# Feed forward of a three-layer fp32 block kernel: gate and up products as seven quarter products and sums, with the weight sums on GpSimd and VectorE

## Chip, cores and metric

One Trainium2 chip, one of its NeuronCores. The metric is the device time of one execution in microseconds (us). Everything is float32. Engines are named as in the profile: PE is TensorE (its weight loads, PEld, are listed apart), DVE is VectorE, ACT is ScalarE, POOL is GpSimd, SP is SyncE, which here issues the weight transfers.

## What is computed

The whole program is two layers of attention, gating and a mixture of experts, then a second kind of block over 256 tokens of width 1024. The change touches the last part of that block alone, the feed forward:

```python
h = rmsnorm(x, pre_ffn_g[l])
gt = causal_dwconv(h @ w_ff_gate[l], ff_conv_w[l]) + ff_conv_b[l]
y = (jax.nn.gelu(gt, approximate=True) * (h @ w_ff_up[l])) @ w_ff_down[l]
x = x + rmsnorm(y, post_ffn_g[l])
```

`h` is 256 tokens by 1024, `w_ff_gate` and `w_ff_up` are 1024 by 2816, `w_ff_down` is 2816 by 1024. The convolution goes over the tokens, with three taps, each column by itself.

## The kernel before, in words

The gate and up weights come in 11 chunks (`UP_CHUNKS`) of 2 MB, each 256 columns of the gate matrix and the 256 columns of the up matrix that belong to them, for all eight 128-row pieces of the depth (`KD`). They go in turn into four ring slots. SP issues the load into a slot when the last product of the chunk that lay there is done (`last_read` in the sync block). The normed tokens lie transposed in `x2T` (128 partitions, 8 depth pieces, 256 tokens).

In `feed_forward` of the tensor block a chunk is four products into four banks of PSUM, `A[0]`, `V[0]`, `A[1]`, `V[1]` (gate and up, for each of two 128-column halves `f`), each of eight matmuls of 256 tokens. An fp32 matmul stands as two PE instructions in the trace, so a chunk is 64 of them. ScalarE copies each gate bank to `gate_in`, VectorE runs three convolution operations per half into `conved` (L3044 to L3046), ScalarE applies the GELU (L2084), and VectorE multiplies by the up bank into `hidden` (L3053). ScalarE loads a table whenever it goes from copying to GELU or back.

After the 11 chunks the down products (L1571) run over `hidden` in six chunks of up to four tiles, into the banks `S[0]`, `S[1]`, `V[2]`, `V[3]`. Ahead of the feed forward stands `mixed_norm`: VectorE norms the rows (L3027, behind a power that GpSimd computes, L3095), PE transposes them (`turn_mixed`, L1302), ScalarE and VectorE write `x2T`. GpSimd has nothing to do during the feed forward; its last two powers belong to the norm at the very end. Each engine runs its own instructions in the order in which they are written, and semaphores alone hold the engines together.

Of the kernel before, what the change touches and what calls it, by code (L numbers as in the profile page):

```python
# [21 lines left out]
P = 128  # L22
# [261 lines left out]
def emit(nc, ctx, t, out):  # L284
# [15 lines left out]
    def count(name):  # L300
        return Count(nc, ctx, name)
# [25 lines left out]
    def col(name, l=None):  # L327
        a, n = COLS_AT[name if l is None else f"{name}{l}"]
        return cols[:, a:a + n]
# [98 lines left out]
    mix_g, ffn_g = heads[:, 5632:6656], heads[:, 6656:7680]  # L428
    gate_in = work[:, 0:2 * (SEQ + 2)].rearrange("p (b n) -> p b n", b=2)
    conved = work[:, 1024:1536].rearrange("p (b n) -> p b n", b=2)  # L430
    wr_flat = wr[:, :, :, :].rearrange("p l k n -> p (l k n)")
    w_alow = wr_flat[:, 0:KD * GLA_RANK].rearrange("p (k n) -> p k n", k=KD)
    w_alpha = wr_flat[0:GLA_RANK, 128:384]
# [109 lines left out]
    o2sq_done = count("o2sq_done")  # L543
    y_gla_done = count("y_gla_done")
    conv_done, gelu_done = count("conv_done"), count("gelu_done")
    x_done = count("x_done")
    dve_step = count("dve_step")
    out_stored = sem("out_stored")
# [3 lines left out]
    names = ("list", "weights", "rows", "pe", "act", "dve", "index", "gate", "sent", "passed")  # L552
    xb = [{n: sem(f"further_{n}{l}") for n in names} for l in range(DEPTH)]
    mark = {}

    def h_done_mix(l):
        return sum(2 * tiles(k) for k in range(l + 1))
# [5 lines left out]
    def at_bank(b):  # L563
        return (b.full, b.fills)

    def let_go(b):
        return (b.free, b.fills)
# [27 lines left out]
    def _(pe):  # L595
        def slot_of(c):
            s, n = AT[c]
            pe.wait_ge(ring_loaded[s], 16 * (n + 1))
            return ring[s]
# [4 lines left out]
        def emptied(*banks):  # L604
            for b in banks:
                pe.wait_ge(b.free, b.fills)
# [688 lines left out]
        def turn_mixed(tile):  # L1295

            for q, b in enumerate((S[tile], V[tile])):
                pe.wait_ge(*((xhat_done.sem, NT * DEPTH + 2 + tile + 1) if q else (xhat_half.sem, 2 + tile + 1)))
                pe.wait_ge(b.free, b.fills)
                for j in range(4):  # L1300
                    f = 4 * q + j
                    mm = pe.transpose(b.t[:, j * P:(j + 1) * P], x2hat[:, tile, f * P:(f + 1) * P], ident)  # L1302
                mm.then_inc(b.full, b.fill())
                mark["mixed_T", tile, q] = at_bank(b)

        def columns2(name, banks, between=None):
            w = slot_of(("in2", 2, name))
# [230 lines left out]
            mark["attended", 2] = at_bank(S[0])  # L1538

        def feed_forward():  # L1540
            mark["up"] = [b.fills for b in A + V]

            def chunk(q, loaded):
                s = AT["up", 2, q][0]
                pe.wait_ge(ring_loaded[s], loaded)
                for f in range(2):
                    for part_, b in ((0, A[f]), (1, V[f])):
                        pe.wait_ge(b.free, b.fills)
                        for k in range(KD):
                            c0 = k * COLS + part_ * 256 + f * P  # L1550
                            mm = pe.matmul(b.t[:, 0:SEQ], ring[s][:, c0:c0 + P], x2T[:, k, :], start=(k == 0), stop=(k == KD - 1))  # L1551
                        mm.then_inc(b.full, b.fill())

            n_turn = UP_CHUNKS // NSLOT
            turns = Turns(*[(b, "fills", NSLOT) for b in (A[0], A[1], V[0], V[1])])
            with pe.Fori(0, n_turn) as i:
                turns.turn(i)
                for q in range(NSLOT):
                    chunk(q, 16 * (AT["up", 2, q][1] + 1) + 16 * i)
            turns.done(n_turn)  # L1560
            for q in range(n_turn * NSLOT, UP_CHUNKS):
                chunk(q, 16 * (AT["up", 2, q][1] + 1))

            down_banks = (S[0], S[1], V[2], V[3])
            mark["down"] = [b.fills for b in down_banks]
            for b in down_banks:
                pe.wait_ge(b.free, b.fills)
            def down(w, k, tile, half):
                b = down_banks[2 * tile + half]
                c0 = k % DOWN_K * D + half * 512  # L1570
                mm = pe.matmul(b.t[:, :], hidden[:, k, tile * P:(tile + 1) * P], w[:, c0:c0 + 512],  # L1571
                               start=(k == 0), stop=(k == FF_TILES - 1))
                if k == FF_TILES - 1:
                    mm.then_inc(b.full, b.fill())
                    mark["summed", 3, tile, half] = at_bank(b)
                return mm

            last = (DOWN_CHUNKS - 1) * DOWN_K
            for c in range(DOWN_CHUNKS - 1):
                w = slot_of(("down", 2, c))  # L1580
                for k in range(c * DOWN_K, (c + 1) * DOWN_K):
                    for tile in range(2):
                        for half in range(2):
                            mm = down(w, k, tile, half)
                mm.then_inc(down_used.sem, down_used.up())
                mark["used", "down", 2, c] = (down_used.sem, down_used.n)
            emptied(V[0], V[1])
            w = slot_of(("down", 2, DOWN_CHUNKS - 1))
            for tile in range(2):
                for half in range(2):  # L1590
                    for k in range(last, FF_TILES):
                        down(w, k, tile, half)
# [32 lines left out]
    def _(act):  # L1625
# [448 lines left out]
            out(len(items) - 1)  # L2074

        def feed_forward():
            turns = Turns((A[0], "reads", 1), (A[1], "reads", 1), (gelu_done, "n", 2))
            with act.Fori(0, UP_CHUNKS) as i:
                turns.turn(i)
                for f in range(2):  # L2080
                    evacuate(A[f], gate_in[:, f, 2:], n=SEQ)
                for f in range(2):
                    act.wait_ge(conv_done.sem, 2 * i + f + 1)
                    nc.scalar.activation(conved[:, f, :], conved[:, f, :], ACT.Gelu_apprx_tanh,  # L2084
                                         bias=col("ff_conv_b")[:, bass.ds(2 * i + f, 1)]).then_inc(gelu_done.sem, gelu_done.up())
            turns.done(UP_CHUNKS)

        act.wait_ge(first_loaded, 32)
        for l in range(DEPTH):
# [30 lines left out]
    def _(dve):  # L2120
        def step(ins):
            ins.then_inc(dve_step.sem, dve_step.up())
            dve.wait_ge(dve_step.sem, dve_step.n)
# [906 lines left out]

        def feed_forward():
            taps = col("ff_conv_w")
            step(nc.vector.memset(gate_in[:, :, 0:2], 0.0))
            turns = Turns((V[0], "reads", 1), (V[1], "reads", 1), (dve_step, "n", 4),
                          (conv_done, "n", 2))
            with dve.Fori(0, UP_CHUNKS) as i:
                turns.turn(i)
                for f in range(2):
                    def tap(k):
                        return taps[:, bass.ds(k * FF_TILES + 2 * i + f, 1)]  # L3040

                    y = conved[:, f, :]
                    dve.wait_ge(A[f].free, mark["up"][f] + i + 1)
                    step(TS(y, gate_in[:, f, 0:SEQ], tap(0), None, ALU.mult))  # L3044
                    step(STT(out=y, in0=gate_in[:, f, 1:SEQ + 1], scalar=tap(1), in1=y, op0=ALU.mult, op1=ALU.add))
                    STT(out=y, in0=gate_in[:, f, 2:SEQ + 2], scalar=tap(2), in1=y, op0=ALU.mult, op1=ALU.add)\  # L3046
                        .then_inc(conv_done.sem, conv_done.up())
                for f in range(2):
                    b = V[f]
                    dve.wait_ge(b.full, b.reads + 1)  # L3050
                    dve.wait_ge(gelu_done.sem, 2 * i + f + 1)
                    dst = hidden[:, bass.ds(2 * i + f, 1), :].rearrange("p k n -> p (k n)")
                    TT(dst, conved[:, f, :], b.t[:, 0:SEQ], ALU.mult).then_inc(b.free, b.read())  # L3053
                    dve.wait_ge(b.free, b.reads)
            turns.done(UP_CHUNKS)

        zero_conditions()
        dve.wait_ge(first_loaded, 32)
# [33 lines left out]
    def _(pool):  # L3092
# [134 lines left out]
        pool.wait_ge(*mark["attended", 2])  # L3227
        for dst, name in ((mix_g, "post_mix_g"), (ffn_g, "post_ffn_g")):
            pool.dma_start(dst, t[name].to_broadcast([P, D])).then_inc(block2_in[1], 16)
        for tile in range(2):  # L3230
            for q in (tile, 2 + tile):
                power(rstd[:, q:q + 1], rstd[:, q:q + 1])
        for tile in range(2):
            power(rstd[:, tile:tile + 1], rstd[:, tile:tile + 1])

# [2 lines left out]
    def _(sp):  # L3238
# [18 lines left out]
        def last_read(c):  # L3257

            kind, l, j = c
            if kind == "up":  # L3260
                return V[1].full, mark["up"][3] + j + 1
            if kind == "expert":
                return expert_read(l, j // 3, (j // 3) % 2, j // 3 // 2, j % 3)
            return mark[("used",) + c]
# [294 lines left out]
```

## Time and profile before

| | |
|---|---|
| median of 3 runs | 2682.75 us (2682.36 to 2684.23) |
| span of the profiled execution | 2678.8 us |
| PE busy | 2482.2 us, 93% of the span |
| DVE busy | 779.4 us, 29% |
| ACT busy | 459.3 us, 17% |
| POOL busy | 169.9 us, 6% |
| gate and up products | 2442.6 to 2594.8 us of the span |
| down products and last norm | 2594.8 to 2678.8 us |

The span is counted from the first to the last instruction of one profiled execution; the time of a run holds 4 us more. Busy shares are means over a program of very different stages. The views that follow look at the feed forward and at its border with the stage ahead of it. A PE instruction is listed with its start and a modelled end; matmuls overlap, so their pace is read from the distance of starts, not from their durations.

### The profile page before, as it was taken

What the parts mean: (1) busy time and instruction counts of PE and PEld (TensorE: products, weight loads), DVE (VectorE), ACT (ScalarE), POOL (GpSimd) and SP (SyncE); (2) the same over time, 40 slices, a digit from 0 to 9 for tenths busy, and PEclk for the clock granted to TensorE, in tenths of its full rate; (3) what the DMA queues carried; (4) which work ended last, traced back from release to release, by engine and by line L of the source; (5) the groups of instructions that cost most, each with busy time, mean ns of one, the idle gap of its engine ahead of it and who ended that gap; (6) DMA issues with size and microseconds to landing.
All of it is one profiled execution on the core that took longest, in us unless ns stands there. A gap on an engine that the chain in (4) does not pass through costs nothing.

```text
span 2678.8 us, 30491 instructions
## 1 busy us (share of the span) xinstructions
PE 2482.2 (93%) x12232; PEld 1517.3 (57%) x12232; DVE 779.4 (29%) x1660; ACT 459.3 (17%) x1043; POOL 169.9 (6%) x193
## 2 busy tenths in 40 slices
PE   9999999999987778799999998877879999999998
PEld 4444454445554444445678655444445688887873
DVE  3694444115311111154353321000003323212210
ACT  2121233101000000022132111000002122102320
POOL 0000000000211111000000012111100000000000
PEclk9999999999999999999999999999999999999999
DMA  8464011425999999954424699999995332334331
GB/s 330 178 236 182 32 64 36 185 94 211 418 424 425 426 426 425 414 237 184 193 95 178 256 401 421 425 425 425 425 409 217 132 126 95 142 147 167 149 145 52
DMA packets 63048, 666.44 MB, mean 249 GB/s; under 512 B 13058, under 2 KB 13346, under 8 KB 24400
## 3 DMA queue, kind: packets, MB, share of 16 engines
q1 hardware_dynamic: 48384, 634.68, 58.0%
q0 software_dynamic: 13392, 24.82, 2.5%
q10 hardware_dynamic: 1152, 5.24, 0.5%
q8 instruction: 87, 1.43, 0.2%
q14 instruction: 33, 0.27, 0.0%
HBM read 664.28 MB, written 21.02 MB: 256 GB/s over the span
## 4 chain that ended last, share of the span: by engine, by line
PE 73%; DMA 21%; issue 3%; DVE 1%; ACT 1%; SPq 0%; POOL 0%; DVEq 0%; ACTq 0%; POOLq 0%
DMA ring<-in_w_moe 9%; PE act_bank L752 7%; PE act_bank L739 7%; PE act_bank L873 6%; DMA xT<-in_w_moe 5%; PE act_bank L1314 5%; PE vec_bank L889 4%; PE score_bank L1174 4%; PE vec_bank L1057 4%; PE vec_bank L1186 4%; PE score_bank L873 4%; PE vec_bank L873 3%; PE act_bank L1551 3%; PE vec_bank L1551 3%; DMA heads<-in_w_moe 3%
## 5 line engine op out<-in xcount | busy, mean ns | idle before, releaser
L752 PE MATMUL act_bank<-xT,ring 128*128 128x512 f32 (+1 forms) x512 | 193.6, 539 | 0.0
L739 PE MATMUL act_bank<-ring,xT 128*128 128x512 f32 x416 | 182.0, 593 | 0.7 <-issue 0.6
L2631 DVE TENSOR_TENSOR heads<-work,vec_bank 128x256 f32<-128x256 f32 x64 | 27.0, 421 | 502.3 <-PE vec_bank L1174 502.3
L873 PE MATMUL act_bank<-xT,ring 128*128 128x256 f32 (+1 forms) x576 | 157.8, 427 | 0.4 <-ACT branches L1631 0.4
L752 PEld LDWEIGHTS act_bank<-xT,ring 128*128 128x128 f32 x512 | 97.0, 190 | 94.6 <-issue 91.4
L1174 PE MATMUL score_bank<-ring,branches 128*64 128x256 f32 x1024 | 122.1, 392 | 21.7 <-issue 13.5
L1186 PE MATMUL vec_bank<-ring,heads 128*64 128x512 f32 x512 | 116.9, 598 | 27.2 <-DMA ring<-in_w_moe 17.6
L1174 PE MATMUL vec_bank<-ring,branches 128*64 128x256 f32 x1024 | 117.2, 381 | 22.8 <-DMA ring<-in_w_moe 22.8
L873 PEld LDWEIGHTS act_bank<-xT,ring 128*128 128x128 f32 x576 | 109.2, 190 | 42.5 <-issue 30.5
L739 PEld LDWEIGHTS act_bank<-ring,xT 128*128 128x128 f32 x416 | 78.0, 190 | 95.8 <-issue 95.8
L1314 PE MATMUL act_bank<-xT,ring 128*128 128x256 f32 x576 | 126.6, 380 | 0.6 <-ACT work L1997 0.6
L889 PE MATMUL vec_bank<-branches,ring 128*128 128x256 f32 (+1 forms) x416 | 125.6, 445 | 0.0
L1174 PEld LDWEIGHTS score_bank<-ring,branches 128*64 128x64 f32 x1024 | 83.1, 141 | 68.8 <-issue 43.9
L1314 PEld LDWEIGHTS act_bank<-xT,ring 128*128 128x128 f32 x576 | 108.7, 190 | 16.7 <-issue 2.2
L3095 POOL TENSOR_TENSOR stat<-stat,const 128x1 f32<-128x1 f32 (+3 forms) x35 | 23.5, 673 | 1431.8 <-DVE stat L2376 474.9
L1896 ACT ACTIVATE work<-score_bank 128x256 f32<-128x256 f32 x64 | 24.6, 384 | 516.7 <-PE score_bank L1174 516.7
L1057 PE MATMUL vec_bank<-ring 128*128 128x512 f32 x256 | 111.7, 593 | 0.0
L1174 PEld LDWEIGHTS vec_bank<-ring,branches 128*64 128x64 f32 x1024 | 75.9, 137 | 61.6 <-DMA ring<-in_w_moe 31.6
L2213 DVE CUSTOM_DVE_ANT_0 ring<-ring,branches 128x1024 f32<-128x1024 f32 x80 | 100.7, 1280 | 21.1 <-DMA ring<-in_w_ada 21.1
L873 PE MATMUL score_bank<-xT,ring 128*128 128x256 f32 (+1 forms) x320 | 106.1, 472 | 0.0
L3143 POOL DMA_INDIRECT y_rows<-work,table x60 | 61.0, 1016 | 708.9 <-DVE work L2698 685.3
L889 PEld LDWEIGHTS vec_bank<-branches,ring 128*128 128x128 f32 x416 | 79.0, 190 | 38.1 <-issue 30.6
(438 smaller groups left out, 3359.0 us busy)
## 6 DMA issues: line engine op xcount, KB each, us to landing
ring<-in_w_moe SPq DMA_DIRECT2D x95, 2048.0 KB, 36.7
ring<-in_w_in SPq DMA_DIRECT2D x29, 2048.0 KB, 9.0
ring<-in_w_merge SPq DMA_DIRECT2D x27, 2048.0 KB, 7.6
branches<-in_w_moe SPq DMA_DIRECT2D x24, 2048.0 KB, 36.5
heads<-in_w_moe SPq DMA_DIRECT2D x24, 2048.0 KB, 36.6
ring<-in_w_ada SPq DMA_DIRECT2D x23, 2048.0 KB, 9.4
values<-in_w_moe SPq DMA_DIRECT2D x23, 2048.0 KB, 36.7
xT<-in_w_moe SPq DMA_DIRECT2D x22, 2048.0 KB, 36.6
```

Source lines behind the costliest of these rows:

```text
L739: mm = pe.matmul(b.t[:, :], xT[:, k, tile * P:(tile + 1) * P], w[:, k * COLS:(k + 1) * COLS], start=(k == 0), stop=(k == KD - 1))
L752: mm = pe.matmul(b.t[:, 0:n], w[:, k * COLS + f * P:k * COLS + (f + 1) * P], xT[:, k, 0:n], start=(k == 0), stop=(k == KD - 1))
L873: mm = pe.matmul(g.t[:, 0:n], merge_tile(l, i, MERGE_TILES * d + k), xs[:, k, 0:n], start=(k == 0), stop=(k == KD - 1))
L889: mm = pe.matmul(y.t[:, 0:n], merge_tile(l, i, MERGE_TILES * d + KD + k), ys[:, BRANCH_ORDER[i], k, 0:n], start=(k == 0), stop=(k == 3))
L1057: mm = pe.matmul(b.t[:, :], merged[l][:, k, tile * P:(tile + 1) * P], w[:, k * COLS:(k + 1) * COLS], start=(k == 0), stop=(k == KD - 1))
L1174: mm = pe.matmul(o.t[g * CAP:(g + 1) * CAP, 0:D_HALF], xgT[:, b, c, half * CAP:(half + 1) * CAP], w[:, c0:c0 + D_HALF], start=(k == 0), st ...
L1186: mm = pe.matmul(o.t[g * CAP:(g + 1) * CAP, :], hidT[:, b, c, half * CAP:(half + 1) * CAP], w[:, c0:c0 + HALF], start=(k == 0), stop=(k == 3))
L1314: mm = pe.matmul(b.t[:, 0:SEQ], w[:, k * COLS + f * P:k * COLS + (f + 1) * P], x2T[:, k, :], start=(k == 0), stop=(k == KD - 1))
L1551: mm = pe.matmul(b.t[:, 0:SEQ], ring[s][:, c0:c0 + P], x2T[:, k, :], start=(k == 0), stop=(k == KD - 1))
L2213: ins = nc.vector.tensor_tensor_reduce(ada_junk if k < ns - 1 else w, w, cond_rows[:, k, :], 1.0, bias, ALU.mult, ALU.add, dst)
L2631: TT(hid[:, b, :], silu_s[:, b, :], V[b].t[:, 0:D_HALF], ALU.mult).then_inc(V[b].free, V[b].read())
L3143: pool.indirect_dma_start(out=half_rows(y_rows[l][0:tiles(l) * 2 * P, :]), out_offset=bass.IndirectOffsetOnAxis(ap=table[:, e:e + 1], axis=0),
```

## The change

Chunk 0 stays as it was. Of each of the chunks 1 to 10 the weights are seen as a 2 by 2 block matrix (gate and up by the two halves of the depth) and the tokens as another (the halves of the depth by the two halves of the tokens). The product of the two, eight quarter products before, is built from seven quarter products of sums (the scheme of Winograd and Strassen): products 1, 2 and 3, 4, 5, 6, 7 in the text below. A quarter product is 4 depth pieces by 2 column halves: eight matmuls of 128 tokens instead of 256, so 16 PE instructions. It fills half of what four banks held, two halves `f` in one bank. The banks alternate between two sets from chunk to chunk.

The sums of tokens are made once, by VectorE (`sum_tokens`). Of each chunk four weight sums of 128 by 1024 elements are needed: three are made on GpSimd (`sum_weights`), one on VectorE (`differ_weights`), a chunk ahead, into two sets of buffers in `branches` and `values`, which are free by then. After the products ScalarE copies product 1 and later the bank that holds products 1 and 2; VectorE forms the rest with five additions of 128 by 256 elements per chunk, each with one input in PSUM and one in SBUF; the up rows then lie in SBUF (`up_rows`) instead of in PSUM. The loops of PE, ScalarE and VectorE over the chunks are written out instead of being loops of the engine. GpSimd begins with the first chunk's sums when its fourth power of `mixed_norm` is done and the last sums of the mix-out product are in.

The diff, cut (`convolve` does what L3044 to L3046 did, with the same shapes):

```diff
+    first_kept, two_sum, three_sum = [work[:, 1536 + 256 * i:1792 + 256 * i].rearrange("p (f n) -> p f n", f=2) for i in range(3)]
+    up_rows = work[:, 2560:3072].rearrange("p (f n) -> p f n", f=2)
+    x_sums = spare.rearrange("p (m k n) -> p m k n", m=4, k=KD // 2)
+    w_sums = [[a.rearrange("p (k n) -> p k n", k=KD // 2) for a in quarters] for quarters in (
+        [branches[:, 1024 * m:1024 * (m + 1)] for m in range(4)],
+        [branches[:, 4096:5120], branches[:, 5120:6144], values[:, 2048:3072], values[:, 3072:4096]])]
...
+            def seven_chunk(i):
+                one, six, seven, five = [(A[0], V[0], V[1], A[1]), (S[0], V[2], V[3], S[1])][i % 2]
+                mark["ff_banks", i] = (one, six, seven, five)
+                sums = w_sums[i % 2]
+                def product(m, b, w, x, first=True):
+                    pe.wait_ge(b.free, b.fills)
+                    for f in range(2):
+                        for k in range(KD // 2):
+                            mm = pe.matmul(b.t[:, f * P:(f + 1) * P], w[:, k, f * P:(f + 1) * P], x[:, k, :],
+                                           start=(first and f == 0 and k == 0), stop=(f == 1 and k == KD // 2 - 1),
+                                           skip_group_check=True)
+                    mm.then_inc(b.full, b.fill())
+                    mark["ff", i, m], mark["ff_free", i, m] = at_bank(b), let_go(b)
+                pe.wait_ge(*up_loaded(i))
+                product(1, one, up_quarter(i, 0, 0), x_quarter(0, 0))
+                pe.wait_ge(x_summed.sem, 4)
+                pe.wait_ge(w_summed.sem, 3 * (i - 1) + 2)
+                product(6, six, sums[1], x_sums[:, 1])
+                pe.wait_ge(w_differed.sem, i)
+                product(7, seven, sums[2], x_sums[:, 2])
+                product(5, five, sums[0], x_sums[:, 0])
+                product(2, one, up_quarter(i, 0, 1), x_quarter(1, 0), False)
+                product(4, seven, up_quarter(i, 1, 1), x_sums[:, 3], False)
+                pe.wait_ge(w_summed.sem, 3 * i)
+                product(3, five, sums[3], x_quarter(1, 1), False)
+                used(("up", 2, i), five)
+            plain_chunk(0)
+            for i in range(1, UP_CHUNKS):
+                seven_chunk(i)
...
+                pe.wait_ge(hidden_done.sem, 4 * c + 2)
...
-            emptied(V[0], V[1])
+            pe.wait_ge(hidden_done.sem, 2 * (UP_CHUNKS - 1))
...
+            for i in range(1, UP_CHUNKS):
+                b = mark["ff_banks", i][0]
+                half = b.t[:, 0:SEQ].rearrange("p (f n) -> p f n", f=2)
+                act.wait_ge(*mark["ff", i, 1])
+                nc.scalar.activation(first_kept, half, ACT.Copy).then_inc(b.free, 1)
+                gelu(i - 1)
+                act.wait_ge(*mark["ff", i, 2])
+                nc.scalar.activation(gate_in[:, :, 2:P + 2], half, ACT.Copy).then_inc(b.free, 1)
+            gelu(UP_CHUNKS - 1)
...
+            def sum_tokens():
+                for tile in range(2):
+                    dve.wait_ge(*mark["mixed_gone", tile])
+                t1, t2, t3, t4 = [x_sums[:, m] for m in range(4)]
+                step(TT(t1, x_quarter(0, 1), x_quarter(0, 0), ALU.subtract))
+                TT(t3, x_quarter(1, 1), x_quarter(0, 1), ALU.subtract)
+                step(TT(t2, x_quarter(1, 1), t1, ALU.subtract))
+                TT(t4, x_quarter(1, 0), t2, ALU.subtract).then_inc(x_summed.sem, x_summed.up(4))
+            def differ_weights(i):
+                dve.wait_ge(*up_loaded(i))
+                if i >= 3:
+                    dve.wait_ge(*mark["ff", i - 2, 7])
+                TT(w_sums[i % 2][2], up_quarter(i, 0, 0), up_quarter(i, 1, 0), ALU.subtract)\
+                    .then_inc(w_differed.sem, w_differed.up())
+            def convolve(i):
...
+            def hide(i):
                 for f in range(2):
-                    b = V[f]
-                    dve.wait_ge(b.full, b.reads + 1)
                     dve.wait_ge(gelu_done.sem, 2 * i + f + 1)
-                    dst = hidden[:, bass.ds(2 * i + f, 1), :].rearrange("p k n -> p (k n)")
-                    TT(dst, conved[:, f, :], b.t[:, 0:SEQ], ALU.mult).then_inc(b.free, b.read())
-                    dve.wait_ge(b.free, b.reads)
-            turns.done(UP_CHUNKS)
+                    dst = hidden[:, 2 * i + f, :]
+                    if i == 0:
+                        dve.wait_ge(*mark["ff", i, 1, f])
+                        TT(dst, conved[:, f, :], V[f].t[:, 0:SEQ], ALU.mult).then_inc(V[f].free, 1)
+                    else:
+                        TT(dst, conved[:, f, :], up_rows[:, f, :], ALU.mult).then_inc(hidden_done.sem, hidden_done.up())
+            step(nc.vector.memset(gate_in[:, :, 0:2], 0.0))
+            sum_tokens()
+            differ_weights(1)
+            for f in range(2):
+                dve.wait_ge(*mark["ff_free", 0, 0, f])
+            convolve(0)
+            for i in range(1, UP_CHUNKS):
+                _, six, seven, five = [b.t[:, 0:SEQ].rearrange("p (f n) -> p f n", f=2) for b in mark["ff_banks", i]]
+                _, b6, b7, b5 = mark["ff_banks", i]
+                dve.wait_ge(*mark["ff", i, 6])
+                dve.wait_ge(*mark["ff_free", i, 1])
+                TT(two_sum, six, first_kept, ALU.add).then_inc(b6.free, 1)
+                dve.wait_ge(*mark["ff", i, 7])
+                dve.wait_ge(*mark["ff_free", i, 6])
+                TT(three_sum, seven, two_sum, ALU.add).then_inc(b7.free, 1)
+                hide(i - 1)
+                if i + 1 < UP_CHUNKS:
+                    differ_weights(i + 1)
+                dve.wait_ge(*mark["ff", i, 5])
+                dve.wait_ge(*mark["ff_free", i, 7])
+                if i > 1:
+                    dve.wait_ge(hidden_done.sem, hidden_done.n)
+                else:
+                    for f in range(2):
+                        dve.wait_ge(*mark["ff_free", 0, 1, f])
+                TT(up_rows[:, :, P:], five, three_sum, ALU.add).then_inc(b5.free, 1)
+                dve.wait_ge(*mark["ff", i, 4])
+                TT(up_rows[:, :, 0:P], seven, two_sum, ALU.add).then_inc(b7.free, 1)
+                dve.wait_ge(*mark["ff", i, 3])
+                TT(gate_in[:, :, P + 2:], five, two_sum, ALU.add).then_inc(b5.free, 1)
+                for m in (2, 3, 4):
+                    dve.wait_ge(*mark["ff_free", i, m])
+                convolve(i)
+            hide(UP_CHUNKS - 1)
...
+        def sum_weights(i):
+            def add(dst, a, b, op):
+                nc.gpsimd.tensor_tensor(dst, a, b, op).then_inc(w_summed.sem, w_summed.up())
+            pool.wait_ge(*up_loaded(i))
+            if i >= 3:
+                pool.wait_ge(*mark["ff", i - 2, 3])
+            s1, s2, _, s4 = w_sums[i % 2]
+            add(s1, up_quarter(i, 1, 0), up_quarter(i, 1, 1), ALU.add)
+            pool.wait_ge(w_summed.sem, w_summed.n)
+            add(s2, s1, up_quarter(i, 0, 0), ALU.subtract)
+            pool.wait_ge(w_summed.sem, w_summed.n)
+            add(s4, up_quarter(i, 0, 1), s2, ALU.subtract)
...
+        pool.wait_ge(*mark["summed", 2, 1, OUT_CHUNKS - 1])
+        for i in range(1, UP_CHUNKS):
+            sum_weights(i)
...
```

## Rows read from the trace of the kernel before

**Rows 1.** Windows: PE, PEld, DVE, ACT, POOL busy, clock, DMA, by stretch.

```profile
core 0: us, PE busy (x) PEld busy (x) DVE busy (x) ACT busy (x) POOL busy (x), PEclk, DMA share, GB/s
2442.60:2594.80 152.20, 152.20 (x705) 134.01 (x706) 37.94 (x87) 47.01 (x66) 0.00 (x0) 1.00 0.39 147
2594.80:2678.80 84.00, 75.52 (x176) 33.08 (x175) 6.27 (x13) 2.76 (x8) 1.10 (x2) 0.97 0.21 75
2456.40:2470.20 13.80, 13.80 (x66) 12.15 (x65) 3.49 (x8) 4.35 (x7) 0.00 (x0) 1.00 0.40 153
```

**Rows 2.** Waits from 2442 to 2600 us: total, times, longest.

```profile
ACT work L1631 <- PE act_bank L1551: 103.2, 22, 6.5
DVE work L3044 <- ACT work L1631: 96.6, 22, 5.3
```

**Rows 3.** Timeline of PE, matmuls of 128 and 256 columns: start, duration.

```profile
268.44 1.06 PE L959 MATMUL vec_bank<-values,work 128*128 128x128 f32 x8
269.34 3.17 PE L873 MATMUL vec_bank<-xT,ring 128*128 128x512 f32 x7
...
2268.86 0.83 PE L1526 MATMUL score_bank<-work,values 128*128 128x128 f32 x6
2269.53 1.46 PE L1498 MATMUL vec_bank<-heads 128*128 128x256 f32 x6
```

**Rows 4.** Timeline of one chunk before, ACT, DVE and SP.

```profile
2453.24 0.39 ACT L1631 ACTIVATE work<-act_bank 128x256 f32<-128x256 f32 x1 [6.52 <-PE act_bank L1551]
2453.64 1.28 ACT L2084 ACT_TABLE_LOAD   x1
2453.78 0.35 DVE L3044 TENSOR_SCALAR work<-work,cols 128x256 f32<-128x256 f32 x1 [5.24 <-ACT work L1631]
2454.28 0.48 DVE L3045 SCALAR_TENSOR_TENSOR work<-work,cols 128x256 f32<-128x256 f32 x1
2454.91 0.48 DVE L3046 SCALAR_TENSOR_TENSOR work<-work,cols 128x256 f32<-128x256 f32 x1
2454.94 1.10 ACT L2084 ACTIVATE work<-work,cols 128x256 f32<-128x256 f32 x2
2455.59 0.42 DVE L3053 TENSOR_TENSOR heads<-work,vec_bank 128x256 f32 x1 [0.20 <-ACT work L2084]
```

**Rows 5.** Groups by form, DVE: one and two inputs in SBUF.

```profile
L2334 DVE TENSOR_TENSOR values<-values,const 128x1024 f32<-128x1024 f32 x4 | 4.9, 1222 | 29.4 <-ACT values L1727 29.4
L2248 DVE TENSOR_TENSOR work<-work 128x512 f32<-128x512 f32 x6 | 4.2, 692 | 0.2
L2274 DVE TENSOR_SCALAR values<-h,stat 128x1024 f32<-128x1024 f32 x8 | 6.0, 753 | 5.4 <-POOL stat L3095 5.4
L2781 DVE TENSOR_SCALAR branches<-branches,stat 128x512 f32<-128x512 f32 x4 | 1.8, 484 | 1.7 <-POOL stat L3095 1.7
```

**Rows 6.** Groups by form, POOL: its powers.

```profile
L3095 POOL TENSOR_TENSOR stat<-stat,const 128x1 f32<-128x1 f32 x26 | 14.4, 554 | 725.8 <-DVE stat L2990 365.4 <-DVE stat L2463 211.0 <-DVE stat L2753 62.7
L3095 POOL TENSOR_TENSOR stat<-stat,const 128x8 f32<-128x8 f32 x1 | 1.6, 1632 | 187.3 <-DVE stat L2936 187.3
```

**Rows 7.** Timeline at the border of norm and feed forward.

```profile
2438.74 0.55 POOL L3095 TENSOR_TENSOR stat<-stat,const 128x1 f32<-128x1 f32 x1 [2.78 <-DVE stat L2990]
2439.33 0.88 DVE L3027 TENSOR_SCALAR values<-h,stat 128x512 f32<-128x512 f32 x2 [0.66 <-POOL stat L3095]
2439.87 0.66 PE L1302 MATMUL score_bank<-const,values 128*128 128x128 f32 x4 [0.35 <-DVE values L3027]
2442.58 0.91 PE L1551 MATMUL act_bank<-xT,ring 128*128 128x256 f32 x3 [0.32 <-issue]
```

**Rows 8.** DMA issues from 2400 us on: line, KB each, us to landing.

```profile
ring<-in_w_up SPq DMA_DIRECT2D x11, 2048.0 KB, 8.3
```

More of the change, by code:

```diff
@@ L545, in emit @@
     conv_done, gelu_done = count("conv_done"), count("gelu_done")
+    x_summed, w_summed, w_differed = count("x_summed"), count("w_summed"), count("w_differed")
+    hidden_done = count("hidden_done")
     x_done = count("x_done")
@@ L554, in emit, with up_quarter, x_quarter, up_loaded @@
     mark = {}
+    def up_quarter(i, row, col):
+        w = ring[AT["up", 2, i][0]][:, :].rearrange("p (k n) -> p k n", k=KD)
+        return w[:, KD // 2 * col:KD // 2 * (col + 1), 2 * P * row:2 * P * (row + 1)]
+    def x_quarter(row, col):
+        return x2T[:, KD // 2 * row:KD // 2 * (row + 1), P * col:P * (col + 1)]
+    def up_loaded(i):
+        s, n = AT["up", 2, i]
+        return ring_loaded[s], 16 * (n + 1)
     def h_done_mix(l):
@@ L1304, in turn_mixed @@
                 mark["mixed_T", tile, q] = at_bank(b)
+                if q == 0:
+                    mark["mixed_gone", tile] = let_go(b)
         def columns2(name, banks, between=None):
@@ L1540, in feed_forward, with plain_chunk @@
         def feed_forward():
[L1541 to L1545, printed above, removed]
+            def plain_chunk(i):
+                pe.wait_ge(*up_loaded(i))
+                s = AT["up", 2, i][0]
                 for f in range(2):
@@ L1552, in chunk @@
                         mm.then_inc(b.full, b.fill())
[L1554 to L1562, printed above, removed]
+                        mark["ff", i, part_, f], mark["ff_free", i, part_, f] = at_bank(b), let_go(b)
@@ new lines, in plain_chunk @@
+                used(("up", 2, i), V[1])
+            def seven_chunk(i):
[11 more added lines that the diff above has]
+                    mark["ff", i, m], mark["ff_free", i, m] = at_bank(b), let_go(b)
+                pe.wait_ge(*up_loaded(i))
+                product(1, one, up_quarter(i, 0, 0), x_quarter(0, 0))
[10 more added lines that the diff above has]
+                used(("up", 2, i), five)
@@ L2076, in feed_forward, with gelu @@
         def feed_forward():
[L2077 to L2081, printed above, removed]
+            def gelu(i):
                 for f in range(2):
@@ L2084, in feed_forward @@
                     nc.scalar.activation(conved[:, f, :], conved[:, f, :], ACT.Gelu_apprx_tanh,
-                                         bias=col("ff_conv_b")[:, bass.ds(2 * i + f, 1)]).then_inc(gelu_done.sem, gelu_done.up())
-            turns.done(UP_CHUNKS)
+                                         bias=col("ff_conv_b")[:, 2 * i + f:2 * i + f + 1]).then_inc(gelu_done.sem, gelu_done.up())
+            for f in range(2):
+                act.wait_ge(*mark["ff", 0, 0, f])
+                nc.scalar.activation(gate_in[:, f, 2:], A[f].t[:, 0:SEQ], ACT.Copy).then_inc(A[f].free, 1)
+            for i in range(1, UP_CHUNKS):
[7 more added lines that the diff above has]
+            gelu(UP_CHUNKS - 1)
         act.wait_ge(first_loaded, 32)
@@ L3032, in feed_forward @@
             taps = col("ff_conv_w")
[L3033 to L3037, printed above, removed]
+            def sum_tokens():
[13 more added lines that the diff above has]
+            def convolve(i):
                 for f in range(2):
                     def tap(k):
-                        return taps[:, bass.ds(k * FF_TILES + 2 * i + f, 1)]
+                        c0 = k * FF_TILES + 2 * i + f
+                        return taps[:, c0:c0 + 1]
                     y = conved[:, f, :]
-                    dve.wait_ge(A[f].free, mark["up"][f] + i + 1)
                     step(TS(y, gate_in[:, f, 0:SEQ], tap(0), None, ALU.mult))
@@ L3055, in feed_forward @@
-            turns.done(UP_CHUNKS)
+                    dst = hidden[:, 2 * i + f, :]
[6 more added lines that the diff above has]
+            sum_tokens()
@@ new lines, in feed_forward @@
+            differ_weights(1)
[19 more added lines that the diff above has]
+                else:
+                    for f in range(2):
+                        dve.wait_ge(*mark["ff_free", 0, 1, f])
[7 more added lines that the diff above has]
+                convolve(i)
@@ L3259, in last_read @@
             kind, l, j = c
-            if kind == "up":
-                return V[1].full, mark["up"][3] + j + 1
             if kind == "expert":
```

## Prediction

> **What bounds the kernel now.** I read the windows first, to see which engine fills the stage. From 2442.60 to 2594.80 us PE is busy for all 152.20 us at a granted clock of 1.00, its upper level (2.4 GHz), while DVE is busy for 37.94 us, ACT for 47.01 us and POOL for none [rows 1]. One chunk is one such stretch of 13.80 us [rows 1], 64 PE instructions, 0.2156 us each, and 11 of them are 151.8 us. Then the waits: ACT waits 103.2 us for PE's banks and DVE 96.6 us for ACT [rows 2]; no row of this stretch has PE waiting for them. The DMA share is 0.39 [rows 1], and a load of 2 MB lands 8.3 us after its issue [rows 8], with four slots: transfers are hidden. So in this stage a microsecond taken from PE is a microsecond of the kernel, until DVE or ACT no longer keep up.
>
> **What PE gains.** Chunks 1 to 10 become 7 x 16 = 112 instructions of 128 columns. Their pace is read from starts: eight of L959 take 269.34 - 268.44 = 0.90 us, and six of L1526 take 2269.53 - 2268.86 = 0.67 us [rows 3], 0.112 us each, with a weight load of 128 columns under every one. That is hardly more than half of 0.2156, so the weight load stays hidden. A product is 16 x 0.1116 = 1.785 us, a chunk 12.5 us, and ten chunks save 10 x 1.3 = 13.0 us. These runs are short. The upper bound for a run of 112 is the whole duration of L959's eight with the end of the last one counted in, 1.06 / 8 = 0.133 [rows 3], as if nothing followed closely; the lower one is half of 0.2156, 0.108 (0.4 us a chunk more to gain). I take 0.1116, what the starts show.
>
> **What DVE and ACT gain in work.** By chunk DVE has: two convolutions, 2455.39 - 2453.78 = 1.61 us each [rows 4], together 3.3; five additions with one input in PSUM at 0.42 (L3053, the same shape, [rows 4]), 2.1; two multiplications into `hidden`, 0.84; one weight difference of 128 x 1024, 1.22 [rows 5]. Sum 7.5 us of 12.5. ACT has two copies of 0.39, two table loads of 1.28 and two GELUs, 1.10 in all [rows 4]: 4.4 us. Both fit. The order matters more than the sum. Time is counted from the end of the previous chunk's product 3, as the banks of a chunk fill at 1.8 (product 1), 3.6 (6), 5.4 (7), 7.1 (5), 8.9 (2), 10.7 (4), 12.5 (3). DVE starts 0.2 later, adds (0.65), convolves to 3.95, adds from product 6 (4.4) and 7 (5.9), multiplies (6.8; ACT's GELU is done by 5), makes the next weight difference (8.0) and reads product 5 (8.4). PE wants product 7's bank back at 8.9, for product 4, and product 5's at 10.7, for product 3. Both are free 3.0 and 2.3 us early: nothing waits, and the stage is 13.0 us shorter. The work after the last chunk (about 5 us) lies under the first five of six down chunks, out of 75.52 us of PE work [rows 1]. The token sums (four of 128 x 512, 0.69 each, [rows 5]) and the first sums of weights lie under chunk 0's 13.8 us. The load of a chunk is wanted about one chunk earlier, by the sums; with 8.3 us to land and four slots that costs nothing. The order of SP's queue is unchanged.
>
> **What GpSimd does.** It makes three sums of 128 x 1024 a chunk, each waiting for the one before. No row shows such an operation. The nearest is DVE's same shape, 1.22 us [rows 5]. GpSimd's own rows are powers: 0.554 us for one column, 1.632 for eight [rows 6], so 0.154 a column and 0.40 fixed; 1024 powers at that rate would be 158 us, an end that says little of an addition. Estimate from both: lower end 0.40 + 1.22 = 1.62, and with two of DVE's passes, one for each input, 0.40 + 2.45 = 2.84. I take the middle, 2.2 us, since nothing favours either end; 3 x 2.2 = 6.6 us fits into 12.5 if the engines don't touch. (The Trainium skill, GPSIMD Engine Reference, "Side-by-side cycle accounting", gives 4497 ns for an addition of 2048 columns; half of it, an estimate, would be 2.25 us. No run here has shown it yet.)
>
> **Whether the two engines touch** decides the sign. DVE's operation with one SBUF input costs 753 - 484 = 269 ns for 512 more columns, the one with two 1222 - 692 = 530 ns [rows 5]. So DVE can move two columns where it has one input, as with a second path to SBUF, which two inputs use up. GpSimd must read by some path too. No GpSimd row here is a wide read beside such a DVE operation; its powers have DVE waiting for them [rows 7]. If the path is shared and held for an instruction, the two engines alternate from 0.2 on: both are released by product 3. GpSimd's first sum runs from 0.2 to 2.4. DVE's first convolution operation then waits until 2.4 and ends at 2.8; the second sum runs 2.8 to 5.0, DVE's second operation 5.0 to 5.5, the third sum 5.5 to 7.7, DVE's third 7.7 to 8.15. The second half's convolution ends at 9.75 instead of 3.95. The additions from products 6 and 7 end at 10.65: PE's product 4 begins at 10.7 instead of 8.9. Two multiplications and the weight difference last to 12.7, the reading of product 5 to 13.1: product 3 begins at 13.15 and ends at 14.95. A chunk costs 14.95 us, 1.15 more than before. That holds for chunks 2 to 9; chunk 1 has its sums long before, and GpSimd has none left to make during chunk 10. Sum: 8 x 1.15 - 2 x 1.3 = +6.6 us. At the border, DVE's L3027 (0.88 us, behind the power that ends at 2439.29) meets the first weight sum, which is released by the same power [rows 7], and half of it waits 2.2 us with PE behind it: +2.1. Together +8.7 us. Every 0.1 us of a GpSimd sum is worth 24 x 0.1 = 2.4 us: at 1.62 the time would be 5 us below before, zero lies at 1.84, at 2.84 it is some 27 us above (chunk 1 is late too).
>
> (The Trainium skill, SBUF — State Buffer, "Who interferes with whom", says that a DVE instruction with two SBUF inputs, or in a two-port mode, and a GpSimd instruction that reads SBUF take turns, each for its whole length. That speaks against this change; no row here tests it. By it the result is the sum just worked out, without it the first rival.)
>
> **Forecast and rivals.** The forecast is the case of turns: span 2678.8 + 8.7 = 2687.5, and the median lies 3.95 above the profiled span, so 2691.5 us. Chance 0.54: the rows on DVE's second path lean to it, and none shows the two side by side.
> First rival, the engines don't hold each other up, or so little that 2.3 us of slack a chunk cover it (only the one-input operations take turns, say): 12.5 us a chunk, 13.0 less, 2669.7 us. For it: DVE busy for a quarter of the stage [rows 1]. Chance 0.36.
> Second rival, GpSimd itself sets the pace: it decides from 12.5 / 3 = 4.2 us a sum on; at 5 us a chunk is 15.3 us and the kernel about +8, 2691 us, with PE waiting at product 6 and DVE not late. Only the far end of its bounds reaches there. Chance 0.04.
> Third rival, PE's narrow instructions don't keep 0.112 us in a long run (supply of instructions, weight loads): from 13.8 / 112 = 0.123 on slower than before; at the bound of 0.133 a chunk is 14.9 and the kernel +11, 2694 us. Both short runs in [rows 3] speak against it. Chance 0.06.
>
> **How the numbers follow.** The turns case's own range is 2678 to 2710 us, the first rival's 2667 to 2672. The range given reaches from the first rival to most of the turns case: 2668 to 2704. About 0.2%, 5.4 us, is what a measurement of this kernel can tell from no change. Faster: 0.36 plus the part of the turns case with sums near 1.6 us, 0.04: 0.40. Same: the turns case with sums of 1.7 to 2.0 us, 0.07. Slower: the rest, 0.53.
>
> **What would show it.** In the profile after: PE's starts within a product 0.112 us apart (wrong if not); the stretch of a chunk 12.5 or about 15 us; GpSimd's three sums and their length; the gaps between L3044-like operations, 0.15 us if nothing waits, and about 2 us, three times a chunk, if the engines take turns; PE waiting for DVE ahead of product 4 (1.7 us) and product 3 (0.7); L3027's successor late by 2 us. The prediction is wrong in its main step if DVE's convolution runs gapless beside GpSimd's sums.

## The result and the profile after

The changed kernel takes 2689.5 us (median of 7 runs, 2686.9 to 2695.5), the kernel before 2682.9 us on the same chips; the ratio is 1.0028, with a 95% interval of 1.0017 to 1.0040. It is slower by about as much as the forecast said (2691.5 us), and clear of the bound of 0.2% with its middle, not with the whole interval. The profiled span went from 2678.8 to 2685.3 us, 6.5 us.

The windows first, of the kernel after: the border, the first products of chunk 0, and one chunk (the columns are those of [rows 1]).

```profile
core 0: us, PE busy (x) PEld busy (x) DVE busy (x) ACT busy (x) POOL busy (x), PEclk, DMA share, GB/s
2440.00:2442.00 2.00, 0.08 (x1) 0.08 (x2) 2.00 (x2) 0.00 (x0) 1.92 (x2) 1.00 1.03 438
2442.00:2444.00 2.00, 0.57 (x4) 0.34 (x4) 2.00 (x1) 1.14 (x4) 2.00 (x1) 0.76 0.99 426
2444.00:2446.00 2.00, 1.59 (x6) 1.50 (x7) 0.79 (x3) 0.00 (x0) 1.92 (x2) 0.50 0.81 344
...
2489.36:2503.53 14.17, 13.01 (x114) 12.65 (x113) 12.05 (x14) 1.67 (x4) 7.11 (x3) 1.00 0.40 149
```

A chunk is now 14.17 us, against 13.80 [rows 1], and DVE is busy in 12.05 us of it. Three operations of the timeline below account for 5.8 of these, by lasting longer than they do alone; its own work is 6.3 us (7.5 in the prediction). The clock column shows the second loss, at the border: PE was busy 0.65 us of the 4 us from 2440 on, and the granted clock falls to 0.50, the lower level (1.2 GHz). Before it stayed at 1.00 there.

The timeline shows where DVE's time goes. One chunk after (start, duration; the weight loads and ACT's lines are left out):

```profile
2489.36 1.95 PE L1587 MATMUL score_bank<-xT,ring 128*128 128x128 f32 x16
...
2489.56 0.42 DVE L3159 TENSOR_TENSOR work<-act_bank,work 128x256 f32<-128x256 f32 x1 [1.78 <-PE act_bank L1587]
2489.67 2.35 POOL L3341 TENSOR_TENSOR branches<-ring 128x1024 f32<-128x1024 f32 x1 [6.91 <-PE act_bank L1587]
2490.08 2.09 DVE L3115 TENSOR_SCALAR work<-work,cols 128x256 f32<-128x256 f32 x1
...
2492.10 2.35 POOL L3341 TENSOR_TENSOR branches<-branches,ring 128x1024 f32<-128x1024 f32 x1
2492.21 2.52 DVE L3116 SCALAR_TENSOR_TENSOR work<-work,cols 128x256 f32<-128x256 f32 x1
...
2494.53 2.41 POOL L3341 TENSOR_TENSOR branches<-ring,branches 128x1024 f32<-128x1024 f32 x1
...
2494.77 2.45 DVE L3117 SCALAR_TENSOR_TENSOR work<-work,cols 128x256 f32<-128x256 f32 x1
...
2497.14 0.34 DVE L3115 TENSOR_SCALAR work<-work,cols 128x256 f32<-128x256 f32 x1
...
2497.52 0.48 DVE L3116 SCALAR_TENSOR_TENSOR work<-work,cols 128x256 f32<-128x256 f32 x1
2498.04 0.48 DVE L3117 SCALAR_TENSOR_TENSOR work<-work,cols 128x256 f32<-128x256 f32 x1
2498.44 0.42 DVE L3141 TENSOR_TENSOR work<-vec_bank,work 128x256 f32<-128x256 f32 x1
...
2498.97 0.42 DVE L3144 TENSOR_TENSOR work<-vec_bank,work 128x256 f32<-128x256 f32 x1
...
2499.45 2.05 PE L1587 MATMUL vec_bank<-xT,ring 128*128 128x128 f32 x16 [0.99 <-DVE work L3144]
2499.97 1.22 DVE L3105 TENSOR_TENSOR branches<-ring 128x1024 f32<-128x1024 f32 x1
2501.11 0.42 DVE L3155 TENSOR_TENSOR work<-score_bank,work 128x256 f32<-128x256 f32 x1
...
2501.67 2.02 PE L1587 MATMUL score_bank<-xT,values 128*128 128x128 f32 x16 [0.18 <-DVE work L3155]
...
2503.53 1.95 PE L1587 MATMUL act_bank<-xT,ring 128*128 128x128 f32 x16
```

The same three operations stand in this chunk twice. Beside GpSimd's sums they last 2.09, 2.52 and 2.45 us, a moment later, with GpSimd done, 0.34, 0.48 and 0.48, as in [rows 4] (0.35, 0.48 and 0.48). A wait for the other engine is not idle time in this view: it is part of the duration. It can't be found in the list of waits, only by comparing the durations of one line. PE then waits for L3144 (the addition that frees product 7's bank) and for L3155 (the one that frees product 5's). Its own pace is as read from [rows 3]: products start 1.79 us apart, 16 instructions of 0.112.

The border, after, to be held against [rows 7]:

```profile
2438.73 0.55 POOL L3203 TENSOR_TENSOR stat<-stat,const 128x1 f32<-128x1 f32 x1 [2.79 <-DVE stat L3046]
2439.24 2.34 POOL L3341 TENSOR_TENSOR branches<-ring 128x1024 f32<-128x1024 f32 x1
2439.31 5.04 DVE L3083 TENSOR_SCALAR values<-h,stat 128x512 f32<-128x512 f32 x2 [0.66 <-POOL stat L3203]
2441.66 2.41 POOL L3341 TENSOR_TENSOR branches<-branches,ring 128x1024 f32<-128x1024 f32 x1
...
2441.92 0.66 PE L1322 MATMUL score_bank<-const,values 128*128 128x128 f32 x4 [2.42 <-DVE values L3083]
...
2444.41 1.11 PE L1322 MATMUL vec_bank<-const,values 128*128 128x128 f32 x4 [1.83 <-DVE values L3083]
...
2447.87 4.61 PE L1572 MATMUL act_bank<-xT,ring 128*128 128x256 f32 x16
...
2452.32 3.62 PE L1572 MATMUL vec_bank<-xT,ring 128*128 128x256 f32 x16
```

L3083 is the old L3027. Its two halves lasted 0.88 us together and now last 5.04: both wait, one sum each. Chunk 0 begins at 2447.87 instead of 2442.58, and its first sixteen PE instructions take 4.45 us (to 2452.32) instead of 3.56, most of them at the lower clock: 0.9 us lost.

### The profile page after: what moved, and what is told of

Read it like the earlier page. It is cut to its first block, busy times and chain, and to the rows that moved or that the text cites. A ratio compares the mean times of both kernels' runs of the same rounds, so it can differ in the third digit from the quotient of the medians.

```text
span 2685.3 us, 31275 instructions
## 1 busy us (share of the span) xinstructions
PE 2479.5 (92%) x12712; PEld 1523.7 (57%) x12712; DVE 866.7 (32%) x1724; ACT 430.6 (16%) x1022; POOL 241.4 (9%) x223
## 4 chain that ended last, share of the span: by engine, by line
PE 70%; DMA 21%; DVE 4%; issue 3%; ACT 1%; SPq 0%; POOL 0%; DVEq 0%; ACTq 0%; POOLq 0%
DMA ring<-in_w_moe 9%; PE act_bank L772 7%; PE act_bank L759 7%; PE act_bank L893 6%; DMA xT<-in_w_moe 5%; PE act_bank L1336 5%; PE vec_bank L909 4%; PE vec_bank L1206 4%; PE score_bank L1194 4%; PE vec_bank L1077 4%; PE score_bank L893 4%; PE vec_bank L893 3%; DMA heads<-in_w_moe 3%; PE vec_bank L1194 2%; PE act_bank L1345 2%
```

## The experiments

I use one measure beside the time, the stage: from the first matmul of chunk 0 to the first down product. It is 152.05 us before (2442.58 to 2594.63) and 153.27 after (2447.87 to 2601.14).

**All weight sums on VectorE** (`e1_all_on_vector`). It separates GpSimd's part from the rest of the change.

```diff
+            def sum_one(i):
+                TT(w_sums[i % 2][0], up_quarter(i, 1, 0), up_quarter(i, 1, 1), ALU.add).then_inc(w_summed.sem, w_summed.up())
...
                 TT(two_sum, six, first_kept, ALU.add).then_inc(b6.free, 1)
+                if i + 1 < UP_CHUNKS:
+                    dve.wait_ge(*up_loaded(i + 1))
+                    sum_one(i + 1)
...
                     differ_weights(i + 1)
+                    sum_two(i + 1)
...
                 TT(up_rows[:, :, P:], five, three_sum, ALU.add).then_inc(b5.free, 1)
+                if i + 1 < UP_CHUNKS:
+                    sum_four(i + 1)
...
-        for i in range(1, UP_CHUNKS):
-            sum_weights(i)
...
```

> All four weight sums of a chunk on VectorE, none on GpSimd: one behind the addition from product 6, two behind the multiplications, one behind the reading of product 5. Theory (VectorE's instructions wait for GpSimd's sums, each for the other's whole length): without GpSimd's sums VectorE has 2 x 1.30 (convolutions) + 5 x 0.42 + 0.75 + 4 x 1.22 = 10.3 us a chunk, no gap of 2 us is left, a chunk costs PE's own 12.5 us, chunk 0 is 13.8 again, and nothing is late at the border: 13 us less than before, 2670 us. Rival (seven products with their copies and additions are themselves too much for the chain, whoever makes the weight sums): VectorE has 3.7 us more to do than in the changed kernel, a chunk stays at 14.2 us or more, the time at or above 2683 us.

Measured: 2669.0 us, ratio to before 0.9946 (0.9933 to 0.9960), the stage 138.95 us. Two chunks of it:

```profile
2470.45:2482.95 12.50, 12.50 (x115) 12.50 (x114) 9.78 (x17) 1.68 (x4) 0.00 (x0) 1.00 0.45 170
2482.95:2495.45 12.50, 12.50 (x114) 12.50 (x113) 9.79 (x17) 1.67 (x4) 0.00 (x0) 1.00 0.44 169
```

PE is never idle, and DVE, with more to do than in the changed kernel, is busy for 9.8 us instead of 12.05. The rival is out: the seven products pay their full 13 us once GpSimd's sums are gone. (DVE's 10.3 us of the expectation were 9.8, as many of its operations start before the one ahead has ended.)

**GpSimd released after the norm** (`e2_after_norm`). It prices the border alone.

```diff
         pool.wait_ge(*mark["summed", 2, 1, OUT_CHUNKS - 1])
+        pool.wait_ge(xhat_done.sem, NT * DEPTH + 4)
```

> The changed kernel, with GpSimd's first weight sum released only when VectorE has normed the last rows ahead of the transposes. Theory: of the 6.5 us between the two profiled spans 5.3 are the two halves of the norm (L3083) that wait at the border and 1.0 the half clock of chunk 0's first matmuls; both go, the chunks 2 to 9 stay at 14.2 us: 6.3 us less than the changed kernel, 2683 us, no different from before. Rival (the late start has another cause, such as transfers or the new order of waits): the first product of chunk 0 starts near 2447.9 us again and the time stays at 2689 us.

Measured: 2683.4 us, ratio to before 1.0002 (0.9993 to 1.0012), the stage 152.31 us.

```profile
2442.32 0.88 DVE L3083 TENSOR_SCALAR values<-h,stat 128x512 f32<-128x512 f32 x2 [0.66 <-POOL stat L3203]
...
2442.86 0.66 PE L1322 MATMUL score_bank<-const,values 128*128 128x128 f32 x4 [0.35 <-DVE values L3083]
...
2443.33 2.35 POOL L3341 TENSOR_TENSOR branches<-ring 128x1024 f32<-128x1024 f32 x1 [1.05 <-issue]
...
2445.48 3.69 PE L1572 MATMUL act_bank<-xT,ring 128*128 128x256 f32 x16 [0.23 <-issue]
```

L3083 lasts 0.88 us again, the matmuls follow 3.16 us behind its start as in [rows 7] (3.25), and the first sixteen take 3.53 us at a granted clock of 1.00. One wait of one engine is worth the 6 us by which the changed kernel was slower. The chunks 2 to 9 still take 14.17 us each. (This profile begins the whole stretch some 3 us later than the others, in the stages ahead, which is why I compare distances.)

**GpSimd writes only** (`e3_write_only`) and **GpSimd reads one input** (`e5_one_input`). The two ask which property of its instructions holds DVE up.

```diff
-                nc.gpsimd.tensor_tensor(dst, a, b, op).then_inc(w_summed.sem, w_summed.up())
+                nc.gpsimd.memset(dst, 0.5).then_inc(w_summed.sem, w_summed.up())
```

> GpSimd's three weight sums replaced by memsets of the same tiles (so three of the four weight sums are left out): it writes and reads nothing. Theory A (what is shared is the path by which an instruction reads a second SBUF input): the convolution's scalar_tensor_tensor (L3116, L3117) last 0.48 us beside a memset, and only the one-input tensor_scalar (L3115, in its two-columns-at-once form) may wait; a chunk costs 12.5 us. Theory B (any GpSimd instruction holds VectorE up): waits three times a chunk, each for about a memset's length. The border: L3083 waits for memsets by both, by less than 2.3 us each.

Measured: 2673.8 us in one run, the stage 138.96 us. With one run the stage says more than the time. A chunk's first convolution and the start of the second, beside the memsets:

```profile
2500.29 1.99 POOL L3341 MEMSET branches<- 128x1024 f32 x2 [9.51 <-PE score_bank L1587]
2500.73 0.66 DVE L3115 TENSOR_SCALAR work<-work,cols 128x256 f32<-128x256 f32 x1
2501.43 0.48 DVE L3116 SCALAR_TENSOR_TENSOR work<-work,cols 128x256 f32<-128x256 f32 x1
...
2501.95 0.48 DVE L3117 SCALAR_TENSOR_TENSOR work<-work,cols 128x256 f32<-128x256 f32 x1
...
2502.34 0.95 POOL L3341 MEMSET values<- 128x1024 f32 x1
2502.35 1.09 DVE L3115 TENSOR_SCALAR work<-work,cols 128x256 f32<-128x256 f32 x1
```

The two-input operations run beside a memset as if it weren't there; L3115, with one input and two columns at a time [rows 5], waits in both places. That is theory A. The border is as expected too: the two halves of L3083 last 2.31 us together, and chunk 0 begins 4.55 us behind their start where it was 3.25 [rows 7].

```diff
-                nc.gpsimd.tensor_tensor(dst, a, b, op).then_inc(w_summed.sem, w_summed.up())
+                nc.gpsimd.tensor_copy(dst, a).then_inc(w_summed.sem, w_summed.up())
```

> GpSimd's three weight sums replaced by copies of their first input (so the sums are left out): it reads one tile and writes one. Theory A (a GpSimd instruction that reads SBUF holds the path of VectorE's second input): all of the first three convolution operations of a chunk wait, L3115, L3116 and L3117, each for about one copy's length, unlike beside the memsets, where the last two lasted 0.48 us. Rival (what holds VectorE up is that GpSimd reads two inputs at once): L3116 and L3117 last 0.48 us beside a copy, as beside a memset. The chunk's length follows from the copy's: 14.2 us at 2.4 us a copy, 12.5 below about 1.8 us.

Measured: 2670.8 us in one run, the stage 138.96 us.

```profile
2497.26 1.04 POOL L3341 COPY branches<-ring 128x1024 f32<-128x1024 f32 x1 [9.19 <-PE score_bank L1587]
2497.68 0.76 DVE L3115 TENSOR_SCALAR work<-work,cols 128x256 f32<-128x256 f32 x1
2498.36 1.04 POOL L3341 COPY branches<-branches 128x1024 f32<-128x1024 f32 x1
2498.48 1.20 DVE L3116 SCALAR_TENSOR_TENSOR work<-work,cols 128x256 f32<-128x256 f32 x1
...
2499.46 1.11 POOL L3341 COPY values<-ring 128x1024 f32<-128x1024 f32 x1
2499.71 1.14 DVE L3117 SCALAR_TENSOR_TENSOR work<-work,cols 128x256 f32<-128x256 f32 x1
```

All three wait, each for what is left of one copy. Reading one input is enough. In the chunks it costs the kernel nothing: the convolution of the first half takes 3.1 us (2497.68 to 2500.77) instead of 1.3, and these 1.8 us fit into the slack of 2.3 us that the prediction found, so PE never waits. At the border the halves of L3083 last 2.41 us, and chunk 0 begins 4.65 us behind their start. (The Trainium skill, SBUF — State Buffer, "Who interferes with whom", says just this: a DVE instruction with two SBUF inputs contends with a GpSimd one that reads SBUF and not with one that only writes, one in a two-port mode with both, and the one that comes second waits in full. The three traces agree, with 2.52, 0.48 and 1.20 us for L3116 beside a sum, a memset and a copy.)

**Two sums on GpSimd, two on VectorE** (`e4_two_on_gpsimd`). The dose.

```diff
                     differ_weights(i + 1)
+                    sum_four(i + 1)
...
-            pool.wait_ge(w_summed.sem, w_summed.n)
-            add(s4, up_quarter(i, 0, 1), s2, ALU.subtract)
```

> GpSimd makes two of the sums of a chunk, VectorE makes two. Theory: two waits of about 2.4 us a chunk instead of three; VectorE's second convolution ends at 6.8 us of the chunk, the additions at 7.7, the multiplications at 8.4, two differences at 10.7, product 5 is read at 11.1, against 10.7 at which PE wants its bank: a chunk costs 12.9 us, the ten together 128.2 instead of 138.4; the border stays late by some 5 to 6 us: 2683 - 8.3 + 6 = 2680 us. Rival (no turns: the chain of VectorE is simply long): one more difference on VectorE makes the chunk longer than 14.2 us.

Measured: 2682.0 us, ratio to before 0.9997 (0.9988 to 1.0006), the stage 146.47 us. The three convolution operations are L3121 to L3123 in this kernel. The first two last 2.09 and 2.53 us, the third 0.48: two waits instead of three. A chunk is 13.33 us (product 1 of two chunks at 2490.01 and 2503.34), not 12.9. PE no longer waits ahead of product 4, and 0.59 us ahead of product 3:

```profile
2500.92 0.42 DVE L3163 TENSOR_TENSOR work<-score_bank,work 128x256 f32<-128x256 f32 x1
...
2501.48 2.02 PE L1588 MATMUL score_bank<-xT,values 128*128 128x128 f32 x16 [0.59 <-DVE work L3163]
```

That addition ends at 11.3 us of the chunk, which I had at 11.1, and PE's restart after it takes another 0.2: the expectation was 0.4 us a chunk short. The direction, the number of waits and the one place where PE is held up are as expected; the rival's longer chunk did not come. The border costs what it did in the changed kernel: the two halves of the norm last 5.04 us again, and the first sixteen PE instructions of chunk 0 take 4.38 us, most of them at the lower clock. So the shorter chunks (6.4 us in all) and the border cancel, and the time is that of before.

**The same sums, moved in time** (`e6_moved`). GpSimd keeps all three sums of full length. They are released when DVE has done its last multiplication of the chunk, and the weight difference goes behind the reading of product 5. GpSimd begins behind the norm, as in `e2_after_norm`.

```diff
                 hide(i - 1)
-                if i + 1 < UP_CHUNKS:
-                    differ_weights(i + 1)
...
                 TT(up_rows[:, :, P:], five, three_sum, ALU.add).then_inc(b5.free, 1)
+                if i + 1 < UP_CHUNKS:
+                    differ_weights(i + 1)
...
                 pool.wait_ge(*mark["ff", i - 2, 3])
+                pool.wait_ge(hidden_done.sem, 2 * (i - 2))
...
+        pool.wait_ge(xhat_done.sem, NT * DEPTH + 4)
```

> The three sums stay on GpSimd, all of them, but they are released by VectorE's last multiplication into hidden of a chunk, and VectorE's weight difference moves behind its reading of product 5; GpSimd begins after the norm as in e2_after_norm. So GpSimd's sums fall where VectorE's operations have one input in PSUM. Theory (only an operation with two SBUF inputs or the two-column form waits): the difference waits until about 9.1 us of the chunk and the next convolution's first operation until about 15 (2.5 of the next chunk), the additions from products 5, 4 and 3 do not wait at all; PE never waits, a chunk costs 12.5 us, the time is 2670 us, as with everything on VectorE. Rival (what counts is how long GpSimd is busy beside VectorE, whatever VectorE does): three waits a chunk remain on the way to products 4 and 3, a chunk stays at 14 us, the time at 2683 us.

Measured: 2669.8 us, ratio to before 0.9951 (0.9937 to 0.9965), the stage 138.95 us, no wait of PE in it.

```profile
2489.00 2.35 POOL L3341 TENSOR_TENSOR branches<-ring 128x1024 f32<-128x1024 f32 x1 [4.43 <-DVE heads L3128]
...
2489.53 0.42 DVE L3153 TENSOR_TENSOR work<-score_bank,work 128x256 f32<-128x256 f32 x1 [0.69 <-PE score_bank L1587]
2489.87 2.57 DVE L3105 TENSOR_TENSOR branches<-ring 128x1024 f32<-128x1024 f32 x1
...
2491.44 3.21 POOL L3341 TENSOR_TENSOR branches<-branches,ring 128x1024 f32<-128x1024 f32 x1
...
2493.10 0.42 DVE L3157 TENSOR_TENSOR work<-vec_bank,work 128x256 f32<-128x256 f32 x1 [0.66 <-PE vec_bank L1587]
...
2494.73 2.35 POOL L3341 TENSOR_TENSOR branches<-ring,branches 128x1024 f32<-128x1024 f32 x1
...
2495.41 1.82 DVE L3115 TENSOR_SCALAR work<-work,cols 128x256 f32<-128x256 f32 x1
```

The additions with an input in PSUM (L3153, L3157) last 0.42 us in the middle of a sum. The difference (L3105) waits and lasts 2.57 instead of 1.22, and the first convolution operation 1.82 instead of 0.35, both where nobody is waiting for them. GpSimd pays too: its second sum lasts 3.21 us instead of 2.35, as it waits for the difference. GpSimd makes the same three sums and is shown busy for longer (7.9 us a chunk against 7.1, the 0.9 us of its own wait included), and the kernel is 20 us faster: 6 of these are the border, as in e2, and 13.4 the chunks (the stage of e2 is 152.31 us, of this run 138.95). So it isn't the amount of GpSimd's work that cost the time, but what DVE was doing meanwhile.

Both e1 and e6 beat the kernel before, by 0.5%; their intervals overlap, and nothing here says which is the better.

## Why the prediction was right, point by point

- **PE's gain.** Right. 16 narrow instructions in 1.79 us over runs of 112, a chunk of 12.5 us wherever PE does not wait, 13 us in all with e1 and e6. The rival of a slower narrow pace is out.
- **DVE and ACT have room.** Right: DVE is busy for 9.8 us of 12.5 with even all the sums on it. Its work in the changed kernel was taken as 7.5 us a chunk and is 6.3 without the waits. A convolution was taken as 1.61 us from first start to last end and measured 1.38 (2497.14 to 2498.52), with starts 0.38 and 0.52 us apart where they were 0.50 and 0.63 [rows 4], and the next operation starts 0.08 us before that end. I put this down to writing out the loop, which I had costed at nothing; no run separates it. ACT has 1.67 us of work a chunk and not 4.4: in this stage it loaded a table 22 times before (1.28 us each), and it does so once in the kernel after, and in e1 and e6. No run shows why, and it moves no term of the sum.
- **GpSimd's sum.** Taken as 2.2 us from bounds of 1.62 and 2.84, measured 2.35 to 2.41. The rival of GpSimd as the pace is out. It needed 4.2 us, which lies outside both bounds of the estimate, though the prediction says that their far end reaches there; and a chunk of 15.3 us comes to 8 x 1.5 - 2 x 1.3 = +9.4 us, not +8.
- **The two engines take turns.** Right as to the mechanism, the three places, and who is then late: product 4, then product 3. PE waits 0.99 and 0.18 us there, where I had 1.7 and 0.7; the chunk is 14.17 us long and not 14.95. Two sizes were off. First the turn: I added the DVE operation's own 0.35 or 0.48 us to each sum. GpSimd's sums in fact start 2.43 us apart, 2.35 of their own and a gap of 0.08, so DVE's short operation adds nothing that can be seen. That is more than the longer sums take back: the third convolution operation ends at 7.86 us of the chunk (8.15 in the prediction). Second, DVE's chain from there to product 3 lasts 4.45 us and not 5.0, as its operations start before the one ahead has ended. The term came to +6.6 us in the sum; measured, it is +0.3 (the ten chunks take 138.46 us after, from 2462.68 to 2601.14, and 138.14 before, from 2456.49 to 2594.63).
- **The border.** The mechanism was right and the term mis-sized: +2.1 us in the sum, 5.3 measured. I let only half of L3027 wait. GpSimd started 0.07 us ahead of DVE, so the first half waited for the first sum and the second half for the second. Then 0.9 us more for the clock, which I had not thought of: PE idle for most of 4 us, then half clock for the first matmuls.
- **The sum.** 6.6 + 2.1 = 8.7 forecast, 0.3 + 5.3 + 0.9 = 6.5 measured, and the span is 6.5 us longer. The errors had opposite directions and nearly cancelled; the total is closer than its parts, and that is luck. With the right length of a sum, 2.37 us, the forecast's own rule of 2.4 us for each 0.1 would have given 2695.6 us, further off.
- **The chances.** The rows of before could not settle whether the engines take turns, and I gave it 0.54. The runs settle it.

## What to carry to other kernels

Before work goes to GpSimd, list what VectorE does in those microseconds: beside operations with an input in PSUM it is free, beside operations with both inputs in SBUF, or in the form that does two columns at a time, the one that comes second waits until the other's instruction is done. Long GpSimd instructions beside a chain of short VectorE ones are the worst case, since each short one can wait for a long one; release them where VectorE's next such operation has slack. Look for it in the profile as one line with two durations, not as a wait, and check where the first moved instruction is released: here that single place cost 6 us, beside the 13.4 us that the turns cost in the chunks.

## What the runs showed of the hardware

- A VectorE operation that waits for GpSimd's access is shown as longer, 2.52 us for 0.48, with no idle time ahead of it, and the other way round: a GpSimd sum of 2.35 us is shown as 3.21.
- On GpSimd a 128x1024 float32 sum of two inputs takes 2.35 us (kernel after), a copy 1.04 (e5), a memset 0.95 (e3). Two inputs cost more than twice one. VectorE takes 1.22 for the sum.
- The change-over is tight: with a VectorE operation of 0.35 to 0.48 us between them, two GpSimd sums of 2.35 us start 2.43 us apart. The gap of 0.08 us stands as well where no VectorE operation takes a turn (e6, 2494.65 to 2494.73). A longer one does show: beside the token sums of 0.69 us in chunk 0, GpSimd's sums last 2.68 us.
- In the kernel after, PE was busy for 0.65 us of the 4 us from 2440 on and then got the lower clock until about 2450 us, 0.9 us lost. In e4 the same: busy for 0.75 us of the 4 us from 2442 on, then 0.50. In e3 and e5 it waited for L3083 twice, 1.0 and 0.5 us and 1.1 and 0.5 us, the granted clock stayed at 1.00, and the first sixteen PE instructions took 3.53 us.
